# Six RMS norms of a two-block transformer kernel: squares summed tile by tile in the stage ahead, the next stage's first four tiles fed row by row, stage fences taken out

## What is computed

```python
def rms_norm(x, g):
    y = x * lax.rsqrt(jnp.mean(x * x, axis=-1, keepdims=True) + 1e-6)
    return y * g
# block 1
x = x + mixed @ w_out
x = x + (gelu(conv(gate)) * conv(val)) @ w_down          # gate, val = rms_norm(x, norm2_g) @ w_up
# block 2, for each of two layers
h = rms_norm(x, g) * (1 + scale) + shift                 # mixer: h @ w_in -> q, k, v, gates, scan inputs
x = x + gate * (merge(attention, scan) @ w_out)
h = rms_norm(x, g_mlp) * (1 + scale2) + shift2
x = x + gate2 * (square(relu(h @ w_mlp1)) @ w_mlp2)
return rms_norm(x, final_g)
```

## Time and profile before

| | us |
|---|---|
| median of 3 runs | 2976.41 (2974.76 to 2976.74) |
| profiled execution: time | 2975.33 |
| profiled execution: span in the trace | 2973.7 |
| TensorE matmuls busy | 2604.5 (88% of the span) |
| TensorE weight loads busy | 2217.8 (75%) |
| VectorE busy | 1290.3 (43%) |
| ScalarE busy | 886.0 (30%) |
| GpSimd busy | 1697.2 (57%) |
| mean granted TensorE clock | 0.941 of full |

### The profile page before, as it was taken

How to read it: one execution, slowest core, us unless ns; L and a number is a source line. 1 busy time by engine, 2 the same in 40 slices (tenths; PEclk the granted TensorE clock), 3 DMA queues, 4 the chain that set the end, 5 groups by cost and what they waited for, 6 DMA issues and landing times. The chain is left out here.

```text
span 2973.7 us, 38582 instructions
## 1 busy us (share of the span) xinstructions
PE 2604.5 (88%) x15355; PEld 2217.8 (75%) x15355; DVE 1290.3 (43%) x2208; ACT 886.0 (30%) x1562; POOL 1697.2 (57%) x1470
## 2 busy tenths in 40 slices
PE   6988997999998898886996999969989888877997
PEld 5668985885787777765875788758867777667997
DVE  2535402237636777673123102131464887724210
ACT  2335522115422222222002102032363333243532
POOL 1008766750356666554875788745225666556775
PEclk9999998999899999997998999989999999979999
DMA  6445452337331121211421333323443222234453
GB/s 168 157 155 162 134 156 65 95 109 242 115 111 51 45 57 42 71 43 57 127 85 57 85 99 95 90 71 100 156 139 107 78 65 70 85 114 142 147 156 107
DMA packets 418067, 312.74 MB, mean 105 GB/s; under 512 B 12384, under 2 KB 415874, under 8 KB 417026
## 3 DMA queue, kind: packets, MB, share of 16 engines
q1 hardware_dynamic: 413120, 297.36, 33.9%
q10 hardware_dynamic: 4226, 12.98, 1.1%
q0 software_dynamic: 576, 0.43, 0.2%
HBM read 303.40 MB, written 7.34 MB: 104 GB/s over the span
## 5 line engine op out<-in xcount | busy, mean ns | idle before, releaser
L2320 POOL TENSOR_TENSOR rounded<-ring,rounded 128x512 fp32r<-128x512 f32 (+1 forms) x872 | 1130.7, 1329 | 706.3 <-ACT rounded L1180 540.7
L680 PE MATMUL PS<-rounded 128*128 128x256 f32 (+1 forms) x7728 | 1316.4, 334 | 156.0 <-DVE rounded L1723 55.6
L680 PEld LDWEIGHTS PS<-rounded 128*128 128x128 f32 x7728 | 1175.8, 195 | 296.5 <-issue 103.2
L2343 POOL TENSOR_TENSOR rounded<-ring,constants 128x512 fp32r<-128x512 f32 x272 | 284.2, 1076 | 360.5 <-PE PS L680 171.9
L983 PE MATMUL PS<-rounded 128*128 128x512 f32 (+1 forms) x1536 | 357.6, 390 | 8.1 <-POOLq L2290 4.4
L983 PEld LDWEIGHTS PS<-rounded 128*128 128x128 f32 x1536 | 280.2, 192 | 71.6 <-issue 9.1
L1180 ACT ACTIVATE rounded<-ring 128x2048 fp32r<-128x2048 f32 (+1 forms) x106 | 192.7, 1827 | 150.4 <-DMA ring<-in_w_mlp_dram 62.1
L2069 DVE SCALAR_TENSOR_TENSOR mid_a<-PS,V,mid_a 128x510 f32<-128x510 f32 (+3 forms) x256 | 182.1, 713 | 74.5 <-ACT mid_a L1473 67.4
L990 PE MATMUL PS<-rounded 128*128 128x256 f32 x1152 | 164.8, 305 | 0.0
L990 PEld LDWEIGHTS PS<-rounded 128*128 128x128 f32 x1152 | 156.6, 208 | 5.8 <-issue 2.4
L2232 DVE SCALAR_TENSOR_TENSOR xT<-PS,mod,xT 128x256 f32<-128x256 f32 x40 | 17.9, 480 | 265.0 <-PE PS L680 265.0
(11 more groups left out here) (221 smaller groups left out, 2978.9 us busy)
## 6 DMA issues: line engine op xcount, KB each, us to landing
ring<-in_w_in_dram SPq DMA_DIRECT2D x64, 1024.0 KB, 5.3
ring<-in_w_mlp_dram SPq DMA_DIRECT2D x64, 1024.0 KB, 5.7
ring<-in_ada_w_dram SPq DMA_DIRECT2D x48, 1024.0 KB, 5.2
ring<-in_w_in_dram SPq DMA_DIRECT2D x65, 512.0 KB, 4.1
ring<-in_w_up_dram SPq DMA_DIRECT2D x44, 512.0 KB, 5.0
ring<-in_w_ssd_o_dram SPq DMA_DIRECT2D x16, 1024.0 KB, 5.7
ring<-in_w_out_dram SPq DMA_DIRECT2D x12, 1024.0 KB, 5.3
ring<-in_w_down_dram SPq DMA_DIRECT2D x16, 704.0 KB, 4.8
```

What stands on the lines that cost most here:

```text
L680: mm = pe.matmul(PS[:, b, 0:cols], w[:, k, m * P:(m + 1) * P], x(half * kt + k), start=(half == 0 and k == 0 and n_pass == 0), stop=(half ...
L2320: ins = pool.tensor_tensor(lo[:, r], raw[:, r], hi[:, r], ALU.subtract)
L2343: ins = pool.tensor_tensor(hi[:, r], raw[:, r], ones[:, 0:1].broadcast_to([P, 512]), ALU.mult)
```

## The change

1. The fences around six norms are gone; the first norm of block 1 keeps its own. Engines order themselves by the counts that were there.
2. `square_of_tile`: ScalarE squares a row block as soon as its tile of the stage ahead has been added to `xT`. `mean_square`: TensorE adds it into bank 4 one tile behind, inside the stage ahead (`one_behind`); only the last one stands between the stages. A one-column root ahead of the last squares loads ScalarE's table.
3. The first two slabs of the next stage are rounded by ScalarE between the squares (for the mixer the second one right after the root), in layer 0 too, and GpSimd makes their low parts there and then (`round_first`, `first_rests`). They have places of their own (`first_q`, `first_mlp`).
4. VectorE makes the low part of row k-1 after it has scaled row k.
5. `side_by_side`: TensorE takes the first four tiles of the next stage together, one bank each: for each row block 12 matmuls (4 tiles, 3 passes) once the row's low part is there. The four tiles end together, and with them the two slabs are given back. Slabs 2 and 3 of the stage are rounded after the rows.
6. VectorE's gains of the mixer's norm are computed ahead of the adds of the stage before (`mods_of_mix`).
7. The final transposes begin after four scaled rows, and the store is four stores of 256 KB, each after its copy.
8. The loops of the second-product stages that now carry ones-matmuls are unrolled.

```diff
-        mix_at = [slabs_at("big2"), slabs_at("big2") + [AT["mid_a"] + SLAB, AT["big1"] + SLAB]]
+        mix_at = [slabs_at("big2"), [AT["mid_a"] + SLAB, AT["big1"] + SLAB] + slabs_at("big2")]
+        first_q = [slabs_at("mid_v"), [AT["mid_a"] + SLAB, AT["mid_a"]]]
         gate_at = [slabs_at("big2"), slabs_at("big2") + [AT["big1"] + 2 * SLAB, AT["big1"] + 3 * SLAB]]
-        mlp_at = [slabs_at("mid_o"), slabs_at("mid_o", "mid_a")]
+        mlp_at = [slabs_at("mid_o"), slabs_at("mid_a") + [AT["mid_o"] + SLAB, AT["mid_o"]]]
+        first_mlp = [[AT["big1"] + 2 * SLAB, AT["big1"] + 3 * SLAB], mlp_at[1][0:2]]
+        out_sq = [view(big1, 0, KT, T), view(mid_v, SLAB, KT, SEQ)]
...
+            res = view(big2, 0, LT, D)
+            for b in range(2):
+                for t in range(LT):
+                    sp.wait_ge(out_ready, b * LT + t + 1)
+                    sp.dma_start(out[0, t * P:(t + 1) * P, b * 512:(b + 1) * 512], res[:, t, b * 512:(b + 1) * 512])\
+                        .then_inc(stored, 16)
+            sp.wait_ge(stored, 16 * 2 * LT)
...
+                def side_by_side():
+
+                    banks = [(tile[0] + m) % 4 for m in range(4)]
+                    for m in range(4):
+                        ring_wait(freed)
+                    parts = []
+                    for k in range(kt):
+                        row_ready()
+                        for m, b in enumerate(banks):
+                            if k == 0 and m % 2 == 0:
+                                parts.append(split_weights(hi_at, lo_at, kt, width, 16 * loads, first_at[m // 2]))
+                            w_hi, w_lo = parts[m // 2]
+                            for n_pass, (w, x) in enumerate(((w_hi, rhs), (w_hi, rest), (w_lo, rhs))):
+                                mm = pe.matmul(PS[:, b, 0:cols], w[:, k, m % 2 * P:(m % 2 + 1) * P], x(k),
+                                               start=(k == 0 and n_pass == 0), stop=(k == kt - 1 and n_pass == 2))
+                            if k == kt - 1:
+                                mm.then_inc(*c.made(tile_ready))
+                    tile[0] += 4
+
+                if row_ready:
+                    side_by_side()
+                    for j in range(2, 4):
+                        work(j, 0)
+                    n -= 4
...
-            def norm(cols):
-
-                for k in range(KT):
-                    pe.wait_ge(*c.need(squares))
-                    mm = pe.matmul(PS[:, 4, 0:cols], ones, hT[:, k, 0:cols], start=(k == 0), stop=(k == KT - 1))
-                mm.then_inc(*c.made(mean_sq))
+            def mean_square(k, sq, cols):
+
+                pe.wait_ge(*c.need(squares))
+                mm = pe.matmul(PS[:, 4, 0:cols], ones, sq[:, k, 0:cols], start=(k == 0), stop=(k == KT - 1))
+                if k == KT - 1:
+                    mm.then_inc(*c.made(mean_sq))
+
+            def one_behind(sq, cols, halves=1):
+
+                def after(n):
+                    k, half = divmod(n, halves)
+                    if k and half == halves - 1:
+                        mean_square(k - 1, sq, cols)
+                return after
+
+            def rows(n=1):
+                return lambda: pe.wait_ge(*c.need(lo_ready, n))
...
-            to_features(4, lambda k: mix1[:, k, :], SEQ, dve_freed)
-            stage()
-            norm(SEQ)
-            pe.wait_ge(*c.need(lo_ready, KT))
+            to_features(4, lambda k: mix1[:, k, :], SEQ, dve_freed, after=one_behind(hT, SEQ))
+            mean_square(KT - 1, hT, SEQ)
             c.skip(scaled, KT)
-            to_features(FFT, lambda k: hm_hi[1][:, k, :], SEQ, dve_freed, loads=2, body=FFT,
+            to_features(FFT, lambda k: hm_hi[1][:, k, :], SEQ, dve_freed, loads=2, body=FFT, row_ready=rows(),
                         rest=lambda k: hm_lo[:, k, 0:SEQ], hi_at=up_at, lo_at=up_rest_at)
             splits[0] = 0
-            to_features(2 * KT, lambda k: ffn_hi[:, k, :], SEQ, dve_freed, kt=FFT // 2, width=P, halves=2,
-                        rest=lambda k: ffn_lo[:, k, :], hi_at=down_at)
-            stage()
+            to_features(2 * KT, lambda k: ffn_hi[:, k, :], SEQ, dve_freed, kt=FFT // 2, width=P, halves=2, body=2 * KT,
+                        rest=lambda k: ffn_lo[:, k, :], hi_at=down_at, after=one_behind(hT, T, 2))
 
 
             for l in range(LAYERS):
-                norm(T)
-                pe.wait_ge(*c.need(shifted, 2 * KT))
+                mean_square(KT - 1, hT, T)
...
-                to_features(4, hi, q_cols, act_freed, **in_parts)
+                to_features(4, hi, q_cols, act_freed, row_ready=rows(), first_at=first_q[l], **in_parts)
...
+                            hi_at=gate_at[l], after=one_behind(out_sq[l], q_cols))
+                mean_square(KT - 1, out_sq[l], q_cols)
                 c.skip(scaled, n_half * KT)
+                first_row = dict(row_ready=rows(n_half), first_at=first_mlp[l])
...
+                        to_features(HIDT // 4, h_of, T, lo_ready, **h_parts, **(first_row if half == 0 else {}))
+                        to_features(KT, hid_of, T, dve_freed, kt=YT, width=P, body=KT, **hid_parts,
+                                    after=one_behind(hT, T) if half else None)
                 else:
-                    to_features(HIDT // 2, h_of, SEQ, lo_ready, **h_parts)
-                    to_features(2 * KT, hid_of, SEQ, dve_freed, kt=YT, width=P, halves=2, **hid_parts)
-                stage()
-
-
-            norm(SEQ)
-            pe.wait_ge(*c.need(scaled, KT))
+                    to_features(HIDT // 2, h_of, SEQ, lo_ready, **h_parts, **first_row)
+                    to_features(2 * KT, hid_of, SEQ, dve_freed, kt=YT, width=P, halves=2, body=2 * KT, **hid_parts,
+                                after=one_behind(hT, SEQ, 2))
+
+
+            mean_square(KT - 1, hT, SEQ)
             turn_begin()
-            for t in range(LT):
-                for b in range(2):
+            for b in range(2):
+                pe.wait_ge(*c.need(scaled, 4))
+                for t in range(LT):
...
+            def square_of_tile(k, sq, cols):
+
+                act.wait_ge(*c.need(dve_freed))
+                if k == KT - 2:
+                    act.activation(spare[:, 0:1], eps[:, 0:1], ACT.Sqrt)
+                act.activation(sq[:, k, 0:cols], xT[:, k, 0:cols], ACT.Square).then_inc(*c.made(squares))
+
+            def round_first(slabs, n, at):
+
+                act.wait_ge(*slab_loaded[slabs[n]])
+                act.activation(view(R, at[n], SLAB), ring[:, slabs[n] % SLOTS, :], ACT.Copy).then_inc(*c.made(round_ready))
...
+            for k in range(KT):
+                square_of_tile(k, hT, SEQ)
+                if k in (3, 5):
+                    round_slab(ups, k // 2 - 1, up_at)
+            root(SEQ)
...
-                norm(T)
-                act.wait_ge(*c.need(mods_ready))
                 s0 = first_slab["q", l]
                 a0 = first_slab["attn_o", l]
                 slabs = [*range(s0, s0 + 16), *range(a0, a0 + 4)]
-                if l:
-                    for n in range(2):
-                        round_slab(slabs, n, mix_at[l])
+                for k in range(6 if l == 0 else 0, KT):
+                    if k == KT - 1:
+                        round_first(slabs, 0, first_q[l])
+                    square_of_tile(k, hT, T)
+                root(T)
+                round_first(slabs, 1, first_q[l])
+                act.wait_ge(*c.need(mods_ready))
...
+                for k in range(KT):
+                    square_of_tile(k, out_sq[l], q_cols)
+                    if k in (3, 5):
+                        round_first(slabs, k // 2 - 1, first_mlp[l])
+                root(q_cols)
...
+                        k, half = divmod(n - HIDT // 2 - 5, 2)
+                        if k >= 0 and half == 0:
+                            square_of_tile(k, hT, SEQ)
+
+            for k in range(6, KT):
+                square_of_tile(k, hT, SEQ)
+            root(SEQ)
...
-            def norm(gain, cols):
+            def norm(gain, cols, rest=None):
 
                 dve.wait_ge(*c.need(rms_ready))
                 step(dve.reciprocal(rstd[:, 0:cols], rms[:, 0:cols]))
@@ -1696,6 +1762,10 @@
                         r = slice(e * SEQ, (e + 1) * SEQ)
                         dve.scalar_tensor_tensor(out=hT[:, k, r], in0=xT[:, k, r], scalar=gain(k, e), in1=rstd[:, r],
                                                  op0=ALU.mult, op1=ALU.mult).then_inc(*c.made(scaled))
+                    if rest and k:
+                        rest(k - 1)
+                if rest:
+                    rest(KT - 1)
...
+            def first_rests(slabs, at):
+
+                for n, hi_at in enumerate(at):
+                    pool.wait_ge(*c.need(round_ready))
+                    rest_in_place(slabs[n] % SLOTS, hi_at, AT["ring"] + slabs[n] % SLOTS * SLAB, SLAB)
+
             stage()
             rests(up_slabs, up_at, body=FFT, lo_at=(FFT // 2) * up_rest_at)
```

(24 more changed lines are left out.)

91 lines of the change are left out of this document (36 added, 55 removed).

## The result

| | before | after |
|---|---|---|
| median, us | 2975.59 (2973.27 to 2976.74, 4 runs) | 2926.40 (2915.05 to 2928.54, 4 runs) |
| profiled execution: span | 2973.7 | 2924.1 |
| TensorE matmuls busy | 2604.5 (88%) | 2612.9 (89%) |
| GpSimd busy | 1697.2 (57%) | 1682.1 (58%) |
| mean granted clock | 0.941 | 0.947 |

The ratio is 0.9828, with a 95% interval from 0.9802 to 0.9854: some 50 us faster, as forecast (2926). But the sum came out right because two misses cancelled. The stages that the change touches won some 57 us, 7 more than forecast, and a stretch of layer 1 that the change leaves as it was lost 7 to the granted clock. The hit to the microsecond is luck besides: of eleven executions of the changed kernel in all, four took 2915 to 2917 us and seven 2926 to 2932, so that a median of four can come out 10 us lower.

The account below looks back on a forecast made before the run. TensorE, in matmuls nearly nine tenths of the time, was taken as the bound, with gains only from its gaps; terms summed to 48.4 us plus 1.5 for covered cold starts, so -50, giving 2926 us, range 2907 to 2944.

Parts of the forecast that it names:

- What bounds it; the fences: TensorE's gaps at five norms, final norm and tail, together 151 us, come from order of work; fences add next to nothing.
- Ones-matmuls: Seven of eight move into the stage ahead, costing 3.2 or 6.2 us where TensorE bounds it, 0.5 in two others.
- case E: More than forecast: waits filled and clock kept up (3 us), clock up in norm2 and MLP 1 (5), contention stops (5): 2913; chance 0.18.
- Norm2: Rows done at T0 + 16.9, then a wait for the first bank until 21.1; gain 4.8 us.
- Mix 0: Layer 0's mixing norm: VectorE contended throughout, rows 3.7 us apart, fed phase done at T0 + 39.4; gain 12.1 us.
- rival C: Heavier contention: each contended instruction costs 1.7 us, GpSimd's slabs stretch to 12.5; mix 0 +4, MLP 0 +3: 2933; chance 0.12.
- MLP 0: Layer 0's MLP norm: six contended instructions, first row at T0 + 14.1, resume at 39.0; gain 8.0 us.
- Mix 1: Layer 1's mixing norm: rows 1.8 us apart, TensorE waits for slab 2 until T0 + 31.1; gain 5.7 us.
- MLP 1 and tail: Layer 1's MLP norm waits for slab 2 until T0 + 19.1, gain 12.6 us; earlier root, transposes and stores gain 6.2.
- rival D: Late weights: TensorE catches up with slabs; MLP 1 loses 5.9 us, norm2 and mix 1 some 3 each: 2938; chance 0.12.
- rival A: Row-by-row pauses keep TensorE at 1.2 GHz through all five fed phases, +54 us: 2980, no difference; chance 0.05.
- Covered cold starts: Slow rows or a late slab hide part of the low-clock start in mix 0, MLP 0 and mix 1: 1.5 us added.

Follow-up runs that it names:

- e6: The kernel before, with each fence's drain, count and wait done twice in a row: 2974.11 us, ratio 1.0007.
- e2: The changed kernel, but TensorE waits for all eight normed rows before the first matmul of the stage behind each norm: 2969.09 us, ratio 0.9991.
- e3: The changed kernel, but GpSimd splits slabs 2 and 3 only after the last row's low part at layer 0's two norms: 2916.11 us, ratio 0.9812.
- e5: The changed kernel with one 1 MB store behind the last copy in place of four of 256 KB: 2917.26 us, ratio 0.9824.
- e7: The changed kernel run again unaltered: 2917.27 us, ratio 0.9821; its profile was of a run above 2930 us.
- e4: The changed kernel with the Gelu's table loaded ahead of it and slab 3 rounded behind the first Gelu: 2911.89 us, ratio 0.9797.
- e11: The changed kernel unaltered, run once more for its profile: 2927.03 us.

## Why the prediction was right, step by step

- **What bounds it; the fences.** Right. The gain is in the order of the work, e6 prices the fences at nothing, and e2 shows that without the rows one by one the time is back at that of the kernel before.
- **Ones-matmuls.** Right in size. The full stages grew by 2.6, 5.5, 5.5 and 2.4 us (forecast 3.2, 6.2, 6.2, 3.2), as six ones-matmuls stand inside a stage and the seventh right behind its last ordinary matmul. In the stages ahead of mix 0 and of the final norm I charged 0.5 us each, and they became 1.6 and 1.7 shorter: the waits for slabs are filled, and the clock fell less in them. This part of case E came true. Its second did not: the clock was 0.50 at the start of norm2's fed phase, behind an idle time of only 3.98 us.
- **First rows.** Forecast at T0 + 5.1, 12.8, 14.1, 12.2 and 5.4 us; measured 5.7 (225.48), 13.4, 14.6, 12.2 and 5.9 us, T0 being the end of the last ordinary matmul (219.8, 439.1, 1555.8, 1937.6 and 2708.1).
- **Norm2.** Resume at T0 + 23.8, forecast 21.1. The row rate was right; the fed phase began at half clock (3.5 us, window above) and so did the matmuls behind the bank's wait. The step "4.9 us to the bank's release" was right; the cold start that it brings was the part not counted. From the start of `w_out` to that of the down projection the kernel won 3.2 us, forecast 4.8; A hit its forecast of 16.4 (16.7 in this profile) because the stage ahead of mix 0 gave 2.1 more.
- **Mix 0.** Fed phase done at T0 + 41.7, forecast 39.4. Rows beside GpSimd came 3.8 to 4.5 us apart (2.44 to 2.94 for two scales, 1.52 to 1.78 for the remainder), where I had 3.7: the contended instruction, 1.22 in my sum, was 1.2 to 1.5 for a scale and 1.5 to 1.8 for the longer remainder. That lies between the forecast and rival C. The exclusive lock of the Trainium skill ("SBUF — State Buffer", "SBUF: two separate sides") would give the sum of both, 1.26 + 0.44 = 1.7 for a scale and 1.26 + 0.69 = 1.95 for a remainder beside GpSimd's remainder; the trace had at most 1.47 and 1.78, so engines beside each other cost less than in turn. e3 shows that this contention spaced the rows: with GpSimd held back they come every 1.5 us.
- **MLP 0.** Resume at T0 + 40.2, forecast 39.0, for the same cause. Part C still won 10.8, not 8.0: the kernel before also paid a cold start here, which my full-rate 22.2 us left out, the ones-matmuls were 0.7 cheaper, and the second product of the MLP's first half ran 1.5 us faster by the clock (88.7 us for 90.2).
- **Mix 1.** Won 8.8, forecast 5.7, the largest miss. ScalarE ended its rows at T0 + 21.4, not 24, since a row cost 1.46 us and not 1.8; so slab 2 was rounded and split sooner, TensorE went on at T0 + 28.3 and not 31.1, and its wait was 2.70 us, not 5. The mis-sized term is the row's pace.
- **MLP 1 and tail.** Resume at T0 + 20.3, forecast 19.1, and for another reason than forecast: slab 2 was ready at T0 + 17.5, but the fed phase, cold at its start, took 13.55 us and not 11.8, and the 0.82 us behind it are a wait for the first bank. T0 to the end of the span went from 19.4 to 13.1 us: 6.3, forecast 6.2; its stores' share of 1.4 is 1.5 in e5. F and G together -20.0, forecast -18.3, but F varies by 5 between profiles. No slab came late (rival D): the next wait is at 2809.2 and lasts 1.8 us (2.07 before).
- **The clock** (rival A). The pauses of 0.4 to 1.3 us between the pieces of mix 0 did not bring it down: 12 matmuls in 3.02 us are 0.25 each, against 0.232 at full rate, and the clock over the first of these pieces was 1.00. The oscillation of the Trainium skill ("TensorE: Matmul & The Clock Gate", "HAM oscillation — how this bites in real kernels") was not seen in the fed phases.
- **Covered cold starts.** No run isolates the 1.5 us that I added for them.
- **Untouched work.** I took it to stay as it was, without a reason for the clock to do so, and E grew by 6.8 us. This and the 6.7 us that the touched parts won beyond the sum of 49.9 are the two misses that cancelled; with E unchanged the profiled execution would have been near 2919. So the 2926 itself is luck by some 7 us; that each norm resumes within 3 us of its forecast is not.

## What to carry to other kernels

When a chain between two stages is the gap, start the next stage on the first piece of it: here taking out the feeding of four tiles row by row gave the whole gain back, while the early sum and the shorter tail by themselves paid only where no helper stood beside the rows. Then look at who runs beside the chain: helpers that were moved up (GpSimd's weight splits) nearly tripled the time of VectorE's rows, and holding them until the chain was done won another 10 us with one wait at each of two norms. Judge such edits by stretches that repeat to a microsecond in the profiles; the whole time of the same kernel moved by 15 us with the clock of a stretch that nobody touched. And look at untouched stretches in several profiles before and after: a shift that returns every time, as in E, may belong to the change.

## What the runs showed of the hardware that was not expected

- The granted clock in the same instructions differs between kernels and between runs of one: 64 matmuls in 7.34 or 13.7 us, and a stretch of layer 0 in 985.6 or 1000.9 us in one kernel.
- The length of an idle stretch does not tell the clock behind it. In the last MLP stage the same work stands behind the same 1.80 us: the granted clock was 1.00 in the kernel after and 0.51 in e7, and the 192 matmuls took 23.29 and 24.80 us. In the kernel before it was 0.53 behind 2.07 us, in e4 1.00 behind 2.49, and in e11 0.61 behind pauses of 1.25 and 0.79 us; in mix 0 such pauses did no harm. First the kernel after, then e7, then the kernel before:

```profile
2811.04:2814.00 2.96, 2.96 (x24) 2.96 (x25) 0.00 (x0) 1.29 (x1) 2.20 (x3) 1.00 1.11 302
```

```profile
2812.10:2815.50 3.40, 3.40 (x16) 3.40 (x17) 0.00 (x0) 1.28 (x1) 2.65 (x3) 0.51 0.87 247
```

```profile
2852.55:2856.00 3.45, 3.45 (x17) 3.45 (x18) 0.00 (x0) 1.01 (x1) 2.69 (x3) 0.53 0.92 253
```

- Two engines beside each other on the same kind of operands: a VectorE scale of 0.44 us took 1.2 to 1.5, a remainder of 0.69 took 1.5 to 1.8, and GpSimd's four instructions 5.9 for 5.0.
- Doubling every fence of four engines changed nothing that 10 runs could show (ratio 1.0007 [0.9988, 1.0026]).
- A table load of ScalarE took 1.28 us and stood bare before the first Gelu; a dummy activation 8 us earlier took it out of the way (e4).
